# A mixture of experts in four units of columns, with seven-product gate blocks in three of them

## The reference, cut to what matters

```python
def swiglu(h, w_gate, w_up, w_down):
    return (jax.nn.silu(h @ w_gate) * (h @ w_up)) @ w_down

def moe_swiglu(h, w_router, w_gate, w_up, w_down):
    ...
    for e in range(N_EXPERTS):
        y = swiglu(h, w_gate[e], w_up[e], w_down[e]).astype(jnp.float32)
        out = out + combine[..., e:e + 1] * y
    return out.astype(h.dtype)
```

## Time and profile before

| | us |
|---|---|
| median of 3 runs | 1529.07 |
| lowest and highest | 1528.86 to 1533.36 |
| the profiled execution | 1528.53 |
| its span | 1526.7 |

### The profile page before, as it was taken

One profiled execution on the slowest core, in us unless ns is written; L12 is line 12 of the kernel. 1 busy time (PEld: TensorE's weight loads), 2 busy tenths in 40 slices (PEclk: granted clock), 3 DMA queues, 4 the chain that ended last, 5 costly groups with the idle time before them and its releaser, 6 DMA issues.

```text
span 1526.7 us, 27999 instructions
## 1 busy us (share of the span) xinstructions
PE 1508.6 (99%) x11888; PEld 1033.6 (68%) x11888; DVE 921.5 (60%) x1533; ACT 497.4 (33%) x741; POOL 25.3 (2%) x39
## 2 busy tenths in 40 slices
PE   9999999999999999999999999999999999999997
PEld 7887788888888878843466566565565665664664
DVE  7778776888787776643824835726528339248211
ACT  5698745444457987420020110100100100201001
POOL 0000000000000000010000000000000000000100
PEclk9999999999999999999999999999999999999999
DMA  9544376555554444499999999999999999999994
GB/s 385 177 162 164 116 248 207 186 184 182 194 179 149 155 166 146 141 364 425 425 410 425 425 417 425 418 416 425 418 420 426 413 425 424 412 425 416 422 425 183
DMA packets 72673, 478.10 MB, mean 313 GB/s; under 512 B 8097, under 2 KB 8353, under 8 KB 45154
## 3 DMA queue, kind: packets, MB, share of 16 engines
q1 hardware_dynamic: 68656, 460.09, 75.8%
q0 software_dynamic: 3456, 15.72, 2.7%
q10 hardware_dynamic: 434, 0.45, 0.1%
HBM read 471.38 MB, written 4.85 MB: 312 GB/s over the span
## 4 chain that ended last, share of the span: by engine, by line
PE 85%; ACT 6%; DVE 5%; DMA 2%; issue 1%; SPq 0%; ACTq 0%; DVEq 0%
PE bank L1508 24%; PE mid L1508 12%; PE turn L1536 11%; PE bank L1233 7%; PE bank L1239 7%; PE bank L1242 7%; PE mid L1536 4%; PE mid L1233 2%; PE mid L1239 2%; PE mid L1242 2%; PE turn L1570 2%; ACT w_hi L586 1%; DVE w_lo L593 1%; DMA wide<-in_e_down 1%; PE mid L1345 1%
## 5 line engine op out<-in xcount | busy, mean ns | idle before, releaser
L1508 PE MATMUL bank<-wide,gT 128*32 128x448 f32 x3624 | 438.5, 539 | 0.0
L1508 PEld LDWEIGHTS bank<-wide,gT 128*32 128x32 f32 x3624 | 221.4, 110 | 131.6 <-issue 22.6
L593 DVE TENSOR_TENSOR w_lo<-raw,w_hi 128x1024 fp32r<-128x1024 f32 x202 | 244.4, 1223 | 93.0 <-ACT w_hi L586 90.6
L1508 PE MATMUL mid<-wide,gT 128*32 128x448 f32 x1824 | 254.2, 539 | 0.0
L586 ACT ACTIVATE w_hi<-raw 128x1024 fp32r<-128x1024 f32 (+1 forms) x202 | 210.2, 1053 | 101.1 <-PE bank L1242 65.5
L1145 ACT ACTIVATE eh<-bank 128x448 f32<-128x448 f32 x48 | 22.6, 544 | 478.3 <-PE bank L1508 478.3
L1536 PE MATMUL turn<-wide,hT 128*32 128x512 f32 x534 | 176.8, 592 | 1.4 <-DVE sums_w L2140 1.4
L1233 PE MATMUL bank<-w_hi,a_hi 128*128 128x512 f32 (+1 forms) x608 | 164.6, 394 | 0.8 <-ACT a_hi L869 0.8
L2219 DVE TENSOR_TENSOR eh<-mid,eh 128x448 f32<-128x448 f32 x32 | 19.8, 620 | 241.2 <-PE mid L1508 241.2
L1508 PEld LDWEIGHTS mid<-wide,gT 128*32 128x32 f32 x1824 | 115.5, 110 | 66.4 <-issue 12.8
L1242 PE MATMUL bank<-w_lo,a_hi 128*128 128x512 f32 (+1 forms) x608 | 157.1, 381 | 2.1 <-DVE w_lo L593 2.1
(11 more groups left out here) (313 smaller groups left out, 1985.0 us busy)
## 6 DMA issues: line engine op xcount, KB each, us to landing
wide<-in_e_in SPq DMA_DIRECT2D x227, 896.0 KB, 12.4
wide<-in_e_down SPq DMA_DIRECT2D x102, 1024.0 KB, 13.6
raw<-in_stream SPq DMA_DIRECT2D x100, 1024.0 KB, 4.8
extra<-in_e_in SPq DMA_DIRECT2D x23, 896.0 KB
extra<-in_e_down SPq DMA_DIRECT2D x10, 1024.0 KB
raw<-in_e_in SPq DMA_DIRECT2D x6, 896.0 KB, 4.5
wg<-in_gates POOLq DMA_DIRECT2D x2, 2048.0 KB, 10.5
table<-y_rows POOLq DMA_DIRECT2D x7, 384.0 KB
```

Source lines behind the costliest of these rows:

```text
L593: nc.vector.tensor_tensor(w_lo[:, h % H, :], raw[:, part % R, lo:lo + HALF], w_hi[:, h % H, :].bitcast(F32), ALU.subtract).then_inc(lo_rea ...
L1508: ins = nc.tensor.matmul((early, late)[m][t_][strip(r), 0:LANE_W], gT[:, kt, strip(t_)], w_[:, r * LANE_W:(r + 1) * LANE_W], start=kt == 0 ...
```

## The change

- **Units.** Hidden columns are split in four units of 512, 1024, 1024 and 1024 columns (`WIDTHS`: 128, 256, 256 and 256 columns per strip). Every part is now 2048 columns wide, 1 MB, gate and up too: a part of the short unit holds four tiles of input channels, a part of the others two. E_PARTS stays 42: 4 + 8 + 8 + 8 input parts and 14 of the second matrix. Weights come from one array, `e_parts`.
- **Order of the parts.** Unit 0, unit 1, unit 2, four parts of the second matrix, unit 3, the other ten.
- **Seven products in the gates** of units 1, 2 and 3 (`SEVEN_UNITS`), in the first seven experts: the 2 x 2 block product of token groups 1 and 2 takes seven blocks in place of eight. This wants four sums of gT (gS, made in `gathered_sums`), four sums of each gate part's weights (26 parts of an expert have sums now, in place of 14, `SEVENS`), and at the end the seven partial products put together (`combine_gate`) before the silu; ACT first copies two of them out of PSUM.
- **Other.** Gating multiplies groups 1 and 2 in one instruction; the fetched rows are turned in three pieces of one group at three places; up results use other PSUM banks, so PE no longer waits for the rows of the expert before at its first up part.

The core of the diff:

```diff
-UNITS_E = 2
-LANE_W = F_EXP // (UNITS_E * LANES)
+WIDTHS = (128, 256, 256, 256)
+UNITS_E = len(WIDTHS)
+LANE_W = max(WIDTHS)
+SEVEN_UNITS = (1, 2, 3)
...
-    out = [("in", u, kt + k, m) for u in range(UNITS_E) for kt in range(0, KT, 2) for m in range(2) for k in range(2)]
-    return out + [("down", d) for d in range(UNITS_E * UNIT_TILES // 2)]
+    def unit(u):
+        pairs = [(0, 1), (2, 3)] if WIDTHS[u] == LANE_W else [(0, 1)]
+        return [("in", u, m, p) for pair in pairs for m in range(2) for p in pair]
...
+    return unit(0) + unit(1) + unit(2) + downs[:4] + unit(3) + downs[4:]
...
+SEVENS = [i for i, part in enumerate(E_ORDER) if part[0] == "down" or part[1] in SEVEN_UNITS and part[2] == 0]
...
+                            if m == 0 and u in SEVEN_UNITS and seven(pas, e):
+                                n = len(SEVENS) * e + SEVENS.index(i)
+                                if p == 0:
+                                    pe.wait_ge(x_sums, 4 * (e + 1))
...
+                                four(early[0][:, 0:P], a11, b11, opens=True)
+                                four(early[0][:, P:2 * P], a12, b21)
+                                four(early[1][:, 0:P], s4, b22, opens=True)
+                                pe.wait_ge(w_second, n + 1)
+                                four(early[1][:, 3 * P:4 * P], s3, t3)
+                                four(early[1][:, 2 * P:3 * P], s1, t1)
+                                four(early[0][:, 2 * P:3 * P], s2, t2, closes=True)
+                                pe.wait_ge(w_sums, n + 1)
+                                four(early[1][:, P:2 * P], a22, t4, closes=True).then_inc(w_sums_used, 1)
...
+                    if seven(pas, e):
+                        gathered_sums(e)
+                        owed = None
+                        for i in range(E_PARTS):
+                            if i in UP_END or i in GATE_END and GATE_END.index(i) in SEVEN_UNITS:
+                                if owed is not None:
+                                    fourth_sum(e, owed)
+                                    owed = None
+                                if i in UP_END:
+                                    gating(e, UP_END.index(i))
+                                else:
+                                    combine_gate(e, GATE_END.index(i))
+                            if 9 <= i < 9 + GROUPS_E:
+                                turn_fetched(e, [i - 9])
+                            if i + AHEAD in SEVENS:
+                                first_sums(e, i + AHEAD)
+                                if owed is not None:
+                                    fourth_sum(e, owed)
+                                third_sum(e, i + AHEAD)
+                                owed = i + AHEAD
```

More of the change, by code:

```diff
@@ L66 @@
 LANES = P // STRIP
-UNITS_E = 2
-LANE_W = F_EXP // (UNITS_E * LANES)
-UNIT_W = LANES * LANE_W
-UNIT_TILES = LANE_W // STRIP
-UNIT_PARTS = 2 * KT
+WIDTHS = (128, 256, 256, 256)
+UNITS_E = len(WIDTHS)
+LANE_W = max(WIDTHS)
+TILES = [w // STRIP for w in WIDTHS]
+TILE_AT = [sum(TILES[:u]) for u in range(UNITS_E)]
+N_DOWN = sum(TILES) // 2
+FIRST_DOWN = [t // 2 for t in TILE_AT]
+SEVEN_UNITS = (1, 2, 3)
 def dense_order():
@@ L282 @@
 STATIC_PARTS = N_HALF // 2
-assert E_PARTS % SLOW == 0 and LANE_W % STRIP == 0 and UNIT_W <= PART
+assert E_PARTS % SLOW == 0 and LANES * sum(WIDTHS) == F_EXP
 WIDE = R + H
@@ L315, with build @@
 V_END = V_ROUTER + KT * EXPERTS
[L320 removed]
+def build(nc, stream, e_parts, gates_w, x_in, norms, consts_in, vecs_in, out, tokens, table):
     with ExitStack() as ctx:
@@ L1503, in experts @@
[L1503 to L1512 removed]
+                            u, m, p = which
@@ new lines, in experts @@
+                            up = (late[0][:, 0:w], late[0][:, LANE_W:LANE_W + w], late[1][:, 0:w])
+                            place = [early[t_][:, 0:w] for t_ in range(GROUPS_E)] if m == 0 else up
+                            kts = PART // (LANES * w)
+                            if w == LANE_W:
+                                own_ = w_.rearrange("p (k n r c) -> p k r n c", k=kts, n=2, r=LANES)
+                            else:
+                                own_ = w_.rearrange("p (k r c) -> p k r c", k=kts, r=LANES)
@@ new lines, in experts @@
+                            for k in range(kts):
+                                kt = kts * p + k
+                                for t_ in range(GROUPS_E):
+                                    for r in range(LANES):
+                                        ins = nc.tensor.matmul(place[t_][strip(r), :], gT[:, kt, strip(t_)],
+                                                               own_[:, k, r], start=kt == 0 and (m, t_) != (1, 1),
+                                                               stop=kt == KT - 1 and (m, t_) != (1, 0))
+                        else:
+                            d = which[0]
+                            if d == 0 and pas:
@@ L1528, in experts @@
+                            first, last = d == 0, d == N_DOWN - 1
+                            if seven(pas, e):
+                                n = len(SEVENS) * e + SEVENS.index(i)
+                                if d in FIRST_DOWN:
+                                    pe.wait_ge(h_sums, 4 * (q0 + u + 1) + e * (4 * UNITS_E))
+                                pe.wait_ge(w_second, n + 1)
+                                t1, t3, t2, t4 = (set_of(n)[:, j, :] for j in range(4))
                                 s1, s2, s3, s4 = (sT[:, j, d, :] for j in range(4))
```

286 lines of the change are left out of this document (170 added, 116 removed).

## The result

The changed kernel takes **1597.57 us** (median of 5 runs, 1596.48 to 1600.59) against 1529.67 for the kernel before: a ratio of 1.044, with a 95% interval of 1.0417 to 1.046. It is slower by 67.9 us, and 29 us above the forecast of 1569. The profiled execution has a span of 1598.1 us.

The account below looks back on a forecast made before the run. PE busy 99%, weights needing 107.4 us per expert against PE's 106.3, and DVE's stretch after each expert were taken as bounds. 1528.5 - 13.2 + 0.5 - 1.4 + 6 x 6.4 + 2.5 + 7 x 1.5 + 3 gave 1569, range 1558 to 1580.

Parts of the forecast that it names:

- other edits: Remaining changes: late DVE 1.5 us per expert; gate combine, row turning, SyncE queue and more PE instructions to fetch 0 each.
- Products: Matrix work on the experts' inputs: 2.39 us per seven-product gate part, 2.59 per up part; -13.2 us over seven experts.
- issue-bound rival: Narrow products on PE limited by issue, gate parts over 3 us without waits: about 1684 us; chance 7%.
- The wait at the boundary: At an expert's fifth part PE waits 4.1 us for gS, then for weight sums: 6.4 us in each of six experts.
- DVE late for the second matrix: After units 2 and 3 gating delays second-matrix weight sums: 0.7 us at each place, 1.5 per expert, between 0 and 3.
- Expert 0, "2.5": First expert: gS follows DVE's picks at 671.4, so the second gate part ends 2.5 us later.
- The last expert: It uses eight products and takes no sums: inputs 72.7 us, +0.5.
- The clock: PE's clock may fall during the idle at six expert boundaries: 0.5 us each, +3 in all.
- that rival: PE's clock falls at every expert boundary, +3 us at each of six: 1580 to 1590 us; chance 12%.
- The transfer in the chain of expert 6: Expert 6's excess time, with a weight transfer in its chain, goes away: -1.4 us.
- none of the five: Rivals: shorter wait 12%, faster 8%, products bound by issue 7%, clock falling at every boundary 12%, seven products saving nothing (+13).
- the wider range: Range for the whole kernel leaving out the faster and issue cases: 1540 to 1592 us.

Follow-up runs that it names:

- small transfers: From expert 1 on each weight transfer brings only its part's first 128 columns: changed kernel 1572.95 us, kernel before 1527.21 us.
- The freed layout: Changed kernel with DVE's sums of gathered rows and first gate weights moved ahead, and only 128 columns per weight transfer from expert 1 on: 1534.09 us.
- four products: Kernel before, each 448-column product on the experts' inputs issued as four of 112 columns: 1845.91 us, ratio 1.2066.
- a burst of 384: Kernel before, four narrow products only in the first n of each 16 input parts, n from 0 to 12 by expert (384 is n = 2): 1620.56 us.
- three products: Kernel before, each 448-column product on the experts' inputs issued as three of 128, 160 and 160 columns: 1703.37 us, ratio 1.114.

## Why the prediction was wrong

**The step that failed** is one line of the other edits: "More PE instructions to fetch: 0, as the DMA has 5 us of air per expert". I looked at the bytes, 1 MB more, and they are nothing. What matters is that each 256 instructions must come before PE has used up the last ones, and that they come slower while weights stream. With whole transfers this costs 1597.57 - 1572.95 = 24.6 us net. Gross it is 50 us more of stops, of which 22 come out of the waits for DVE, 20 of them for gS.

**Point by point.**
- Products: 2.39 for a gate part and 2.59 for an up part, both as worked out. The issue-bound rival (gate parts over 3 us without waits) is out. PE does start narrow products close together; it is not fed with them quickly enough.
- The wait at the boundary, "6.4 per expert", 38.4 in all, with 3 for the clock: measured 38.9 with the clock in it (1572.95 - 1534.09), when nothing covers it. The mechanism was right, and the size by some luck: the waits for DVE were 28.1 us in place of 38.4 (3.6 at the fifth part in place of 4.1, and 1.1 for weight sums behind it in place of 2.3), and PE's slower products 16.0 in place of 3. The two errors nearly cancel, and so the 1573 so near to 1569 is no proof of the terms. In the kernel as it is, the stops in the short unit cover it: taking it away changed 1597.6 to 1601.9.
- DVE late for the second matrix, "1.5 per expert": with small transfers and the sums moved ahead, the waits at L1607 are 3.5 us in all, not 10.5, and an expert takes 105.3 (from one first second-matrix row to the next):

```profile
933.58 2.80 PE turn L1607 x25
...
1038.88 2.80 PE turn L1607 x25
```

  My products come to 104.5, so 0.8 is lost per expert in place of 1.5, and 1.0 won against the 106.3 before.
- Expert 0, "2.5": its transfers are whole in every run, and stops for instructions cover its wait too (2.19 us at 671.23 and 1.12 at 679.21 in the chain of after). The freed layout stays 6.9 us behind although its six middle experts win about 1.0 each, so its ends lose some 13. By their first products, expert 0 takes 114.7 us in place of 105.5, where I had put 2 more; 6.9 of the 9.2 are stops without a releaser. The last expert takes 2.7 us more in place of 0.5, which is not taken apart.
- The clock: I took 0.5 at each boundary and gave 12% to a fall at every one. In the kernel after it falls four times; with small transfers it falls at each boundary where PE waits 3.6 us, for 6.8 us. There that rival held, at 16.0 us in all (2.7 a boundary, 3 forecast), inside the 38.9 above.
- The transfer in the chain of expert 6, "-1.4": the kernel before gains 1.7 us with small transfers (1528.87 to 1527.21, by one run), and its expert 6 takes 106.3 in place of 107.8.
- Rivals: the direction was right, and none of the five named the cause. The time is 5.6 us above the wider range, and this one term costs 24.6.

The Trainium skill has a rule on this, on the page "Runtime: NRT & Kernel Launch", section "Instruction fetch mechanics": instructions are streamed in blocks of 16 KiB (256 instructions) while the engine works, crossing into the next is "mostly hidden", and the engine issues more slowly than the blocks are filled. The packets of q8 have this size. The rest holds at 21 and 43 instructions per us and fails at 60 and above: 45 stops in the changed kernel, 138 with four products. The page also gives PE room for 2048 instructions, and in another sentence two blocks for "the IRAM"; a burst of 384 already stops PE, which agrees with the second at most; 2048 is contradicted.

## What to carry to other kernels

Cutting products into narrower ones costs little on PE itself (busy 5.7 us longer with two in place of one), but count the instructions per microsecond (each fp32 product on PE is two products and two loads): here 43 came without a stop, though by little, and 60 to 85 did not, once more than about 200 stood in a row. Look for "issue" idle in the middle of a stream, and for the instruction queue beside it; stops that all begin at the same place of a block of 256 instructions are stops for instructions. When an edit that should remove a wait gains nothing, see whether another stop has eaten the wait before: only with that one gone does the edit show its price. A total that comes out near the forecast proves no term of it; here two terms were 10 and 13 us off and nearly cancelled.

## What the runs showed of the hardware

- Instructions arrive in packets of 256, at closest 3.2 to 3.3 us apart (some 77 per us). In the changed kernel, with 389 GB/s on the DMA engines, a PE that has to stop takes 4.5 to 7.0 us from entering one block to going on in the next, and goes on 1.2 to 1.6 us after the packet has landed.
- The stops begin at one place of the instruction stream: all 45 of the changed kernel, 100 with three products and 138 with four begin 193 behind a multiple of 256.
- The supply isn't steady: PE got 49 per us when it wanted 64, and 55 when it wanted 85. Why less at the lower rate stays open; the weights came at 354 GB/s in the first and 317 in the second.
- The load of the DMA engines works by degrees: 4, 18, 28 and 45 stops at 34, 206, 330 and 389 GB/s. The packet's own time hardly changes (0.9 to 1.0 us with four products, whole or small transfers), so the delay lies ahead of its start; how it comes about is open.
- Less than 400 instructions are in store for PE: a burst of 192 at 85 per us passes, one of 384 stops for 1.9 to 3.0 us in all.
